# A gated linear recurrence stage: when weight units are split, when one result is formed, and where the last input sigmoids are written

## The reference, cut to what matters

```
u      = conv4(h @ w_in[:, rec]) + conv_b          # 4 taps, per channel
gate   = gelu(h_x @ w_in[:, gelu])                 # tokens only
for d in (0, 1):                                    # two directions
    r    = sigmoid(u @ w_a[d] + b_a[d])
    i    = sigmoid(u @ w_i[d] + b_i[d])
    a    = exp(coef[d] * r)
    b    = sqrt(1 - a*a) * i * u                    # in the kernel: (1+a) * sqrt(tanh(..)) * i * u
    y_d  = scan: y_t = a_t * y_(t-1) + b_t          # forwards for d = 0, backwards for d = 1
out    = ((y_0 + y_1) * gate) @ w_out               # summed over the five blocks
x      = x + gate_col * rms_norm(out)               # and then the layer's MLP
```

## Time and profile before

| | |
|---|---|
| median of 3 runs | 1676.56 us (1670.72 to 1677.47) |
| profiled execution, its own time | 1678.59 us |
| its span, first to last instruction | 1676.9 us |
| mean granted TensorE clock | 0.969 |
| TensorE matmuls busy | 1563.2 us (93%) |
| VectorE busy | 1103.0 us (66%) |
| ScalarE busy | 846.2 us (50%) |
| recurrent stage in the span | about 669 to 848 us |

### The profile page before, as it was taken

The page is one execution under the profiler, slowest core; times in us unless marked ns, Lnnn a source line. Parts: engine busy times, 40 slices in busy tenths (PEclk is TensorE's granted clock), DMA queues, the critical chain, the costliest instruction groups (busy, mean ns, idle before and its releaser), DMA issues.

```text
span 1676.9 us, 23997 instructions
## 1 busy us (share of the span) xinstructions
PE 1563.2 (93%) x8710; PEld 1285.3 (77%) x8710; DVE 1103.0 (66%) x1741; ACT 846.2 (50%) x1349; POOL 14.0 (1%) x36
## 2 busy tenths in 40 slices
PE   6989989999999999999779999988887899999999
PEld 4855548988888889887569998875666788889788
DVE  3446654854444448699986667875663779687895
ACT  4325545733222227788674445544241657566572
POOL 2000000000000000000010000000000000000000
PEclk9999999999999999999899999997998899999999
DMA  9388732423233232333345665442220579788792
GB/s 346 95 332 295 276 152 76 151 76 96 92 100 100 88 100 76 101 100 103 124 137 178 188 187 163 139 138 80 72 75 0 201 266 369 262 304 320 248 369 97
DMA packets 195800, 279.70 MB, mean 167 GB/s; under 512 B 12434, under 2 KB 111220, under 8 KB 190588
## 3 DMA queue, kind: packets, MB, share of 16 engines
q1 hardware_dynamic: 194308, 274.21, 48.4%
q0 software_dynamic: 1152, 4.19, 0.7%
q10 hardware_dynamic: 248, 0.09, 0.0%
HBM read 277.40 MB, written 1.05 MB: 166 GB/s over the span
## 4 chain that ended last, share of the span: by engine, by line
PE 73%; DVE 14%; ACT 6%; issue 4%; DMA 2%; SPq 1%; DVEq 0%; ACTq 0%
PE bank L435 64%; DVE weights_lo L408 3%; ACT weights_hi L396 2%; PE bank L736 1%; PE bank L1346 1%; PE bank L1330 1%; DMA ada_rows_in<-in_ada_w_dram 1%; PE bank L1314 1%; ACT work L2071 1%; DVE softmax_cols L2582 1%; DMA stage<-in_w_in_dram 1%; DVE work L2573 1%; DVE work L2715 1%; DVE x_and_ctx L582 1%; PE bank L1731 1%
## 5 line engine op out<-in xcount | busy, mean ns | idle before, releaser
L408 DVE TENSOR_TENSOR weights_lo<-stage,weights_hi 128x1024 fp32r<-128x1024 f32 x332 | 394.6, 1220 | 70.9 <-ACT weights_hi L396 67.3
L396 ACT ACTIVATE weights_hi<-stage 128x1024 fp32r<-128x1024 f32 x332 | 338.0, 1055 | 156.0 <-PE bank L435 104.2
L435 PE MATMUL bank<-act_hi,weights_hi 128*128 128x256 f32 (+1 forms) x1040 | 326.4, 314 | 3.3 <-DVE weights_lo L408 2.8
L435 PE MATMUL bank<-act_lo,weights_hi 128*128 128x256 f32 (+1 forms) x1040 | 324.6, 312 | 0.0
L435 PE MATMUL bank<-act_hi,weights_lo 128*128 128x256 f32 (+1 forms) x1040 | 324.5, 312 | 0.0
L435 PE MATMUL bank<-weights_hi,ff_hi 128*128 128x512 f32 x560 | 220.2, 393 | 4.3 <-DVE ff_lo L2927 1.9
L435 PE MATMUL bank<-weights_hi,ff_lo 128*128 128x512 f32 x560 | 219.8, 392 | 0.0
L435 PE MATMUL bank<-weights_lo,ff_hi 128*128 128x512 f32 x560 | 219.4, 392 | 0.0
L435 PE MATMUL bank<-weights_hi,act_hi 128*128 128x512 f32 (+1 forms) x488 | 197.1, 404 | 20.2 <-DVE act_lo L2780 12.7
L435 PEld LDWEIGHTS bank<-act_hi,weights_hi 128*128 128x128 f32 x1040 | 199.9, 192 | 16.9 <-DVE weights_lo L408 3.7
L435 PEld LDWEIGHTS bank<-act_lo,weights_hi 128*128 128x128 f32 x1040 | 200.0, 192 | 11.1
(11 more groups left out here) (393 smaller groups left out, 1990.0 us busy)
## 6 DMA issues: line engine op xcount, KB each, us to landing
stage<-in_mlp_w_dram SPq DMA_DIRECT2D x128, 512.0 KB, 4.0
stage<-in_w_dram SPq DMA_DIRECT2D x96, 512.0 KB, 6.1
ada_rows_in<-in_ada_w_dram SPq DMA_DIRECT2D x40, 1024.0 KB, 5.6
x_and_ctx<-in_w_dram SPq DMA_DIRECT2D x48, 512.0 KB, 6.0
work<-in_w_dram SPq DMA_DIRECT2D x48, 512.0 KB, 6.4
stage<-in_w_in_dram SPq DMA_DIRECT2D x32, 512.0 KB, 4.1
stage<-in_lru_w_in_dram SPq DMA_DIRECT2D x20, 512.0 KB, 3.8
stage<-in_attn_w_qkv_dram SPq DMA_DIRECT2D x12, 512.0 KB, 8.1
```

The source lines that it names most:

```text
L396: act.eng.activation(whi[u % NRING][:], landing(act, u)[:], ACT.Copy).then_inc(sem("hi_ready"), 1)
L408: dve.eng.tensor_tensor(wlo[u % NRING][:], landing(dve, u)[:], whi[u % NRING][:].bitcast(F32), ALU.subtract).then_inc(sem("lo_ready"), 1)
L435: m = pe.eng.matmul(ps, l, r, start=start and j == 0, stop=stop and j == 2, skip_group_check=True)
```

## The change

It moves work within the lists of ScalarE, VectorE and (for banks only) TensorE:

- `lru_a(0)` and `lru_conv(0)` are followed by four splits instead of two. From there on the splits run two units ahead of before: the gates of block n+1 are split with block n's scans still to come.
- The splits that stood behind block 3 on ScalarE and behind `lru_conv(4)` and `lru_d1(3)` on VectorE are spread anew over what follows; the last four on VectorE stand behind `lru_out(4)`.
- `lru_out(0)` stands before the fourth block's `lru_d1(3)` and scans, and not behind them.
- The last block's four input sigmoids are written to two other buffers (`turn` and the free one of U) directly behind `lru_b(3)`, so they don't wait for the scans of block 3. `lru_d1(4)` reads them from there in two instructions of half the size.
- The output sums stand in banks 0 to 3 and the two gate rows in banks 4 to 7.

The diff, cut at lines that only repeat:

```diff
-                      "n1b": ([0, 1, 2, 3],), "n2": ([0, 1, 2, 3], [0, 1, 2, 3]),
+                      "n1b": ([4, 5, 6, 7],), "n2": ([0, 1, 2, 3], [0, 1, 2, 3]),
...
+        LAST_I = [tbuf[:], U[1]]
...
-                    mm = three(pe, psum[4 + 2 * n + tt][:], wh[:, kk, :], wl[:, kk, :], yh[:, tok], yl[:, tok],
+                    mm = three(pe, psum[2 * n + tt][:], wh[:, kk, :], wl[:, kk, :], yh[:, tok], yl[:, tok],
...
-            spread_pe(pe, "g1a", colG, 1, [0, 1], ("gate_col", 3))
-            spread_pe(pe, "g1b", colH, 1, [2, 3], ("gate_col", 4))
+            spread_pe(pe, "g1a", colG, 1, [4, 5], ("gate_col", 3))
+            spread_pe(pe, "g1b", colH, 1, [6, 7], ("gate_col", 4))
...
                 if n >= 2:
                     lru_gelu(n)
-                split_hi(act, 2 if n == 0 else 4)
+                split_hi(act, 4)
+
+            def lru_last_i():
+                n = RB - 1
+                s.wait_ge(sem("u_used"), n)
+                for md in range(4):
+                    c = (md % 2) * 10 + 2 * n + md // 2
+                    s.wait_ge(*act.filled(("i", n, md)))
+                    s.activation(LAST_I[md // 2][:, md % 2, :], plan.bank(("i", n, md))[:], ACT.Sigmoid,
+                                 bias=params[:, 2, 70 + c:71 + c]).then_inc(*act.free(("i", n, md)))
 
             def lru_b(n):
                 for m, kind, dst, col in ((0, "a", R, 50), (0, "i", I, 70), (1, "a", R, 50), (1, "i", I, 70)):
+                    if n == RB - 1:
+                        if kind == "i":
+                            continue
+                        split_hi(act, 2)
                     if n and kind == "a":
...
                 lru_b(n)
-                split_hi(act, 2 if n < RB - 2 else 6 if n == RB - 2 else 4)
+                if n == RB - 2:
+                    lru_last_i()
+                else:
+                    split_hi(act, 2 if n < RB - 2 else 4)
...
-                split_lo(dve, 2 if n == 0 else 4)
+                split_lo(dve, 4 if n < RB - 1 else 0)
 
             def lru_d1(n):
+                if n == RB - 1:
+                    for md in range(4):
+                        v.wait_ge(*dve.freed(("i", n, md)))
+                    for m in range(2):
+                        v.tensor_tensor(I[:, 2 * m:2 * m + 2, :], LAST_I[m],
+                                        U[n % 2][:, m, :].unsqueeze(1).to_broadcast([P, 2, 512]),
+                                        ALU.mult).then_inc(*dve.mark("u_used" if m else None))
+                    v.wait_ge(*dve.own())
+                    v.wait_ge(sem("lru_decay"), 4 * n + 4)
+                    v.scalar_tensor_tensor(out=I, in0=A, scalar=1.0, in1=I, op0=ALU.add,
+                                           op1=ALU.mult).then_inc(*dve.mark())
+                    v.wait_ge(*dve.own())
+                    return
...
-            for n in range(RB):
-                if n + 1 < RB:
-                    lru_conv(n + 1)
-                else:
-                    for j in range(RB - 1):
-                        lru_out(j)
-                        if j % 2:
-                            split_lo(dve, 2)
+            for n in range(RB - 1):
+                lru_conv(n + 1)
+                if n == RB - 2:
+                    lru_out(0)
+                    split_lo(dve, 2)
                 lru_d1(n)
-                split_lo(dve, 2)
+                if n < RB - 2:
+                    split_lo(dve, 2)
                 lru_d2(n)
+            split_lo(dve, 2)
+            lru_out(1)
+            lru_d1(RB - 1)
+            lru_out(2)
+            split_lo(dve, 2)
+            lru_out(3)
+            split_lo(dve, 2)
+            lru_d2(RB - 1)
             lru_out(RB - 1)
-            split_lo(dve, 2)
+            split_lo(dve, 4)
```

More of the change, by code:

```diff
@@ L1498, in _ @@
                         if kp == 0:
-                            if plan.uses[4 + 2 * n + tt]:
-                                t.wait_ge(*pe.bank_free(4 + 2 * n + tt))
-                            pe.take(("lo", n, tt), 4 + 2 * n + tt)
+                            if plan.uses[2 * n + tt]:
+                                t.wait_ge(*pe.bank_free(2 * n + tt))
+                            pe.take(("lo", n, tt), 2 * n + tt)
                         mm = lru_out_mm(n, tt, kp, wh, wl)
                     unit_end(pe, mm)
-            spread_pe(pe, "g1a", colG, 1, [0, 1], ("gate_col", 3))
-            spread_pe(pe, "g1b", colH, 1, [2, 3], ("gate_col", 4))
+            spread_pe(pe, "g1a", colG, 1, [4, 5], ("gate_col", 3))
+            spread_pe(pe, "g1b", colH, 1, [6, 7], ("gate_col", 4))
             u0, views = pe.unit, []
```

## The result

The changed kernel took **1681.47 us** (median of 12 runs, 1679.15 to 1687.66), the kernel before beside it 1676.64 (12 runs, 1670.72 to 1679.28): ratio 1.0041, 95% interval 1.0029 to 1.0053. That is 0.41% slower. Forecast were 1682.9 and a ratio of 1.004.

A forecast was written before the change was run, and what follows sets the result against it. TensorE's length plus its waits bounds the kernel, with VectorE's closed chain deciding behind the 12.20 us wait. 0.5 plus 5.8 gives +6.3 on 1678.59, 1684.9; less 2.0 for the runs' lower median, 1682.9 us, range 1672 to 1688.

The forecast's parts named there:

- Part 1: Blocks 1 to 4, splits two units ahead: weight waits of 4.35 us go, but only 0.3 us gained to `lru_conv(4)`'s end.
- the bank's loop: Loop through ScalarE, VectorE and bank 3, 29.2 us per block, as long as the block, so TensorE waits there instead.
- Four instead of two splits around `lru_conv(0)`: At block 0, ScalarE and VectorE wait for TensorE there, so the extra splits cost 0, at most 1 us.
- The rival that the weight waits are worth what they show: Blocks give 4.35 us instead of 0.3 if the bank's loop is not tight: 1678.9 us; chance 0.12.
- Part 2: VectorE up to block 3's scans: they end at 807.8 against 812.39, with splits and a 2.26 us wait moved out.
- Part 3: Behind block 3's scans: VectorE waits 6.7 us through `split_hi` of 121; last result at 842.3 against 841.79, +0.5 us.
- TensorE's pieces: Sign: TensorE's 12 us wait ahead of the output product splits into three, about 1, 5 and 8 us.
- Part 4: Last four splits behind `lru_out(4)`: 126 and 127 load late, holding the squares; root +6.3 us, 5.8 of it the load.
- the slower rival: Loads issued in a bunch take up to 6.7 us, delaying 121 and 127: +10.0, 1686.6 us; chance 0.17.
- The sum: Whole change: 0.5 for the last result plus 5.8 for the late load, +6.3 us.
- TensorE's idle time ahead of the turning: Sign, ahead of the turning for the MLP: TensorE idle some 10 us instead of 4 to 6.
- The rival that the 12.20 us pay: Units 121 and 127 land hidden, so removing the wait before the output product pays: 1667.6 us; chance 0.06.

The follow-up runs named there:

- ahead_only: The kernel before with only the splits two units ahead from the first block on, nothing else of the change; 1671.87 us, ratio 0.9975.
- roots_last: To both: in blocks 0 to 2 ScalarE's two high splits stand ahead of the square roots instead of behind them; 1669.83 us, ratio 0.9950.
- exps_first: The changed kernel with ScalarE's high splits of units 120 and 121 moved from between block 4's sigmoids to behind its roots; 1675.25 us, ratio 0.9999.
- squares_first: The changed kernel with ScalarE's high splits of units 126 and 127 moved behind the squares and the norm's root; 1677.71 us, ratio 1.0016.
- low_between: The changed kernel with VectorE's low splits of units 122 and 123 between the halves of block 4's scans; 1679.01 us, ratio 1.0021.
- ahead_roots: To ahead_only: high splits of blocks 0 to 2 ahead of the square roots, nothing else of the change; 1668.89 us, ratio 0.9953.
- both: The changed kernel with the edits of squares_first and exps_first together; 1672.62 us, ratio 0.9981.

## Why the prediction came out right

The forecast counts from the profile before, so 0.4 of each time below was there ahead of the stage; it is named where it matters.

**Part 1 (the bank's loop)** was right in its mechanism. Weight waits of 4.35 us went, and waits for L2732 came; ahead_only shows it alone, and roots_last shows that the loop ties the blocks. A gain of 0.3 us was forecast up to the end of `lru_conv(4)`, and it was a loss of 0.4: it ended at 790.47 against 789.73, less the 0.4 from ahead of the stage. The blocks behind block 0 did gain, by 0.5; what was mis-sized is "Four instead of two splits around `lru_conv(0)` [...] 0, at most 1". TensorE began the next product 0.8 us later there, nearly all of it the wait of 0.72 at 702.87. The reason given, that ScalarE waits for TensorE there, covered 0.3 us; that the two extra splits would wait for loads was not in it. The rival that the weight waits are worth what they show falls: in ahead_only, where they are gone too, the blocks end as before.

**Part 2** forecast the end of the scans at 807.8, and it was 808.94: 1.1 late, 0.4 from ahead of the stage and 0.7 from Part 1. ahead_only shows what fewer splits and the wait of 2.26 us less are worth at the root if nothing behind takes it back: 4.2 us.

**Part 3** said that `split_hi` of 121 starts at 814.85 and VectorE waits 6.7. It was 816.16 and 6.99, so Part 2's 1.1 went through and 0.2 came on top. The last result came at 843.58, forecast 842.3. exps_first shows the cause. TensorE's pieces were 1.07, 4.64 and 5.95 (forecast about 1, 5 and 8). The last is shorter because the clock was at 0.77 from 812 to 842: TensorE took 8.6 us for pair 1, against the 5.5 of the forecast at full clock. The 2.4 us of slack that Part 3 left it were just used up: the last pair started at 844.85, right behind the broadcast, with unit 122 there at 844.8. So the clock cost nothing here; in roots_last, where it fell in the last pair, it cost 1.5.

**Part 4** gave +5.8 for the late load. Between the last result and the root the changed kernel lost 5.7, so the sum is right. Removing the hold gives less: squares_first 4.9, and low_between 3.5 with 1.3 of its own cost. In squares_first the squares wait for the last pair, until 846.2, which begins 1.3 us behind the last result and not 0.2 as before, because unit 122 is split only there; this takes the rest. `split_hi` of 127 started at 851.05, forecast 849.8, and the root at 853.29, forecast 852.1. Loads of the four units from 843.5 on took, from issue to landing, 4.1 to 6.8 us with a median of 5.8:

```profile
stage<-in_mlp_w_dram SPq DMA_DIRECT2D x4, 512.0 KB, 5.8
```

The bunch did form, as the slower rival said, but the two loads that ScalarE waited for were its first two, and no more than the forecast was lost. The fit in the Trainium skill's "SBUF — State Buffer" (The DMA setup-cost knee), about 2 us plus bytes at 436 GB/s, makes an estimate of 3.2 us for 512 KB. This trace disagrees: the quickest of the four took 4.1, and the measurement decides.

**The sum** at the root was forecast +6.3 and was +7.1 from the stage's start; by the ratio +6.9. The difference is the 0.7 of Part 1 and the 0.2 of Part 3, less 0.1 in Part 4. The forecast was not right by luck: no large error is hidden by another. TensorE's idle time ahead of the turning was forecast at some 10 us:

```profile
859.61 0.45 PE L500 MATMUL bank<-ident,work 128*128 128x128 f32 x1 [9.01 <-DVE work L591]
```

The rival that the 12.20 us pay falls by ahead_roots: 9.74 us of that wait are left in it, and it is as fast as roots_last, which starts the output product 8.5 us sooner.

## What to carry to other kernels

Where an engine runs its list strictly in order, a step that waits for a load stands for everything behind it: trace each such step back to what issues its load, and if that is later than before, add up what is queued behind it. A wait that can be seen (1.4 us in each block, 12.2 before the output product) is worth nothing while a loop or another engine's chain of the same length runs beside it; lay the loop out and sum it, and shorten that instead. Here moving two splits ahead of two roots on ScalarE gave 2.7 us (from both) and 3.3 us (from ahead_only) at the root, and by the ratios 5.2 and 3.7. The whole mended change gave 4.3, and ahead_only, three edited lines, gave 4.2.

## What the runs showed of the hardware

- Two profiled executions can differ later in the program by where the half clock falls: +7.5 us at the end of the stage was +1.8 at the end of the span, with the granted clock 0.90 against 0.95 from 1030 to 1170. They can differ ahead of the change too: the eleven kernels reached the turning at L500, behind the same lists, between 664.08 and 665.56. The shift between two common instructions, one on each side of the stage, agreed best with the ratio of many runs.
- Two loads that were issued 1.1 us apart let their splits start 2.0 to 2.3 us apart (813.90 and 816.16; 848.99 and 851.05), so the second of a pair cost ScalarE another 1.0 to 1.2 us of waiting.
- Half clock cost time where other engines waited for the stretch, and none elsewhere: with a granted clock of 0.68 in the last pair the root came 5.2 us behind its start (roots_last), at 1.00 it was 3.8 (both); the 0.77 from 812 to 842 in the changed kernel cost nothing at the root.
- A table load took 1.28 us, and the first exponential began 0.01 us behind it (818.39 and 819.68).
